# Streaming block with 64 routed experts: the expert sort is issued ahead of the shared expert, and the kinds of expert take another order

## What is computed

```
scores = sigmoid(t @ w_router)                      # 256 tokens x 64 experts
sel = scores + router_bias
grp_score = sum(top_k(sel in 8 groups of 8, 2))     # the best 4 groups may be used
idx = top_k(where(group allowed, sel, -inf), 8)     # 8 experts for each token
w = scores[idx] / sum(scores[idx]) * 2.5
out = (silu(t @ ws_gate) * (t @ ws_up)) @ ws_down   # shared expert, every token
for e in range(64):
    hid = silu(t @ we_gate[e]) * (t @ we_up[e])     # 1024 -> 256
    out = out + gates[:, e] * (hid @ we_down[e])    # 256 -> 1024
```

## Time and profile before

| | |
|---|---|
| median of 3 runs | 725.2 us (724.77 to 726.61) |
| the profiled execution, its own time | 724.93 us |
| its span, first to last instruction | 723.2 us |
| PE busy | 653.7 us, 90% |
| DVE, ACT, POOL busy | 294.0, 133.1, 38.8 us |
| mean granted TensorE clock | 0.985 of full |
| DMA | 250.70 MB, mean 347 GB/s |

### The profile page before, as it was taken

How to read it: one execution, slowest core, us unless ns; L and a number is a source line. 1 busy time by engine, 2 the same in 40 slices (tenths; PEclk the granted TensorE clock), 3 DMA queues, 4 the chain that set the end, 5 groups by cost and what they waited for, 6 DMA issues and landing times.

```text
span 723.2 us, 11178 instructions
## 1 busy us (share of the span) xinstructions
PE 653.7 (90%) x4223; PEld 380.0 (53%) x4223; DVE 294.0 (41%) x780; ACT 133.1 (18%) x282; POOL 38.8 (5%) x220
## 2 busy tenths in 40 slices
PE   0479999999978889999999999999999999999992
PEld 0448877844534454545545455554555545555541
DVE  4649987596462133233132331332323323232115
ACT  3501122121501111111111111111111111111112
POOL 7000000001100000000000000000000000000000
PEclk9999999999989999999999999999999999999996
DMA  7998789614419787999999999999999999999941
GB/s 238 395 389 323 246 323 411 255 58 175 174 58 421 284 320 282 421 423 420 420 420 421 420 419 420 421 420 421 420 420 420 419 421 420 422 419 420 421 202 60
DMA packets 46008, 250.70 MB, mean 347 GB/s; under 512 B 4673, under 2 KB 7809, under 8 KB 20993
## 3 DMA queue, kind: packets, MB, share of 16 engines
q1 hardware_dynamic: 44434, 248.59, 84.9%
q10 hardware_dynamic: 1520, 1.39, 0.6%
HBM read 248.91 MB, written 1.05 MB: 346 GB/s over the span
## 4 chain that ended last, share of the span: by engine, by line
PE 70%; DVE 17%; DMA 8%; ACT 2%; issue 1%; ACTq 1%; SPq 0%; DVEq 0%
PE PS L1517 10%; PE PS L1513 10%; PE PS L1496 9%; PE PS L1523 8%; DVE MOD L854 7%; PE PS L1571 5%; PE PS L1545 5%; PE PS L1549 5%; DMA ring<-in_w_ada_dram 5%; PE PS L1554 4%; DMA ring<-in_we_up_dram 3%; PE PS L1567 3%; PE PS L1532 2%; PE PS L1314 1%; PE PS L1442 1%
## 5 line engine op out<-in xcount | busy, mean ns | idle before, releaser
L1169 DVE SCALAR_TENSOR_TENSOR arena<-arena,gate,PS 128x128 f32<-128x128 f32 (+1 forms) x48 | 18.0, 375 | 172.6 <-ACT arena L769 172.6
L1314 PE MATMUL PS<-hT,ring 128*128 128x256 f32 x384 | 84.7, 380 | 0.0
L1517 PE MATMUL PS<-ring,arena 128*64 128x256 f32 x704 | 84.6, 391 | 0.0
L1180 DVE TENSOR_TENSOR YLO<-PS,YHI 128x512 fp32r<-128x512 f32 x58 | 40.1, 691 | 101.5 <-ACT YHI L780 101.5
L1314 PEld LDWEIGHTS PS<-hT,ring 128*128 128x128 f32 x384 | 72.5, 190 | 11.1 <-issue 1.6
L1496 PE MATMUL PS<-G,H2HI 128*128 128x256 f32 (+2 forms) x272 | 71.1, 297 | 7.8 <-ACT arena L760 7.2
L1513 PE MATMUL PS<-ring,arena 128*128 128x512 f32 x160 | 73.7, 612 | 0.7 <-issue 0.7
L854 DVE SCALAR_TENSOR_TENSOR MOD<-ring,ccol,MOD 128x768 f32<-128x768 f32 (+2 forms) x72 | 66.9, 930 | 12.5 <-ACT MOD L646 6.8
L780 ACT CAST YHI<-PS 128x512 fp32r<-128x512 f32 x58 | 34.0, 586 | 176.7 <-PE PS L1549 71.0
L1496 PE MATMUL PS<-G,H2LO 128*128 128x256 f32 (+2 forms) x272 | 66.2, 279 | 0.0
L1517 PEld LDWEIGHTS PS<-ring,arena 128*64 128x64 f32 x704 | 47.6, 134 | 31.9 <-issue 3.7
(11 more groups left out here) (255 smaller groups left out, 630.5 us busy)
## 6 DMA issues: line engine op xcount, KB each, us to landing
ring<-in_we_gate_dram SPq DMA_DIRECT2D x64, 1024.0 KB, 14.9
ring<-in_we_up_dram SPq DMA_DIRECT2D x64, 1024.0 KB, 18.1
ring<-in_we_down_dram SPq DMA_DIRECT2D x64, 1024.0 KB, 15.9
ring<-in_w_ada_dram SPq DMA_DIRECT2D x5, 3072.0 KB, 11.3
ring<-in_w_in_dram SPq DMA_DIRECT2D x3, 3072.0 KB, 18.0
ring<-in_w_ada_dram SPq DMA_DIRECT2D x4, 1536.0 KB, 16.0
ring<-in_w_out_dram SPq DMA_DIRECT2D x1, 3072.0 KB, 18.6
ring<-in_w_ada_dram SPq DMA_DIRECT2D x1, 2048.0 KB, 26.6
```

What stands on the lines that cost most here:

```text
L1180: dve.tensor_tensor(y_part(YLO, p, h), bank(5), y_part(YHI, p, h).bitcast(F32), ALU.subtract).then_inc(ylo_ready, 1)
L1314: mm = pe.matmul(PS[:, 2 + q % QB, 0:TOK], w[:, k, (m % 6) * P:(m % 6) * P + P], hT[:, k, :], start=(k == 0), stop=(k == KD - 1))
L1517: m = pe.matmul(PS[64 * c:64 * c + 64, 6, 0:FE].rearrange("p (a n) -> p a n", a=2), xt[:, k, :], gu_cols(w[0], k, c), start=(k == 0), stop ...
```

## The change

Four things are edited.

1. **Router and sort move forward.** On PE the second half's logits go ahead of the last eighth of `shared_gate_up(0)` and of the modulation rows; the counts (`rank_ps`) go into the middle of `shared_gate_up(1)`, and the matmul of the sort stands ahead of both `shared_down`. On ACT the sigmoid goes ahead of the first silu. On DVE the gate values, formerly between mask and ranks, go behind the sort, and `shared_hidden(1)` too.
2. **Units.** The two fixed wide experts are each followed by a pair (two units [wide, pair]); in the other units the wide expert comes last. The same kinds and numbers of positions remain.
3. **Ring.** A slot is handed on in the order in which the positions use it, and the start order of slots is 2, 3, 0, 4, 1 in place of 2, 3, 0, 1, 4.
4. **POOL.** It copies all `rankm` columns of a unit first, then (for the first unit after the new semaphore `rt_ready`) all `RT` columns, and reads the expert number from `order` once for either, twice in all.

Three of the four gather steps of the first unit now stand ahead of `shared_down(1)`.

```diff
-UNITS = ([[WIDE] * FIXED, [PAIR, PAIR]]
-         + 2 * (2 * [[WIDE, PAIR, NARROW], [WIDE, NARROW, PAIR], [NARROW, PAIR, NARROW]] + [[NARROW, PAIR, NARROW]])
+UNITS = (FIXED * [[WIDE, PAIR]]
+         + 2 * (2 * [[PAIR, NARROW, WIDE], [NARROW, PAIR, WIDE], [NARROW, PAIR, NARROW]] + [[NARROW, PAIR, NARROW]])
          + [[NARROW, NARROW]])
...
+PROC = [q for qs in EXPERTS for q in qs]
+POS_OF = [p for q in range(NE) for p in range(NPOS) if q in EXPERTS[p]]
+SLOT, USE = [2, 3, 0, 4, 1], [1] * NSLOT
+for q in range(NSLOT, NE):
+    SLOT.append(SLOT[PROC[q - NSLOT]])
+    USE.append(USE[PROC[q - NSLOT]] + 1)
... SP
                 if q >= NSLOT:
-                    sp.wait_ge(gu_done, POS_OF[q - NSLOT] + 1)
+                    sp.wait_ge(gu_done, POS_OF[PROC[q - NSLOT]] + 1)
... POOL
             for i in range(len(UNITS)):
-                if staged(i):
+                if i:
                     pool.wait_ge(slot_ps, i)
-                    for u, q in enumerate(of_unit(i)):
-                        col = bass.ds(pool.value_load(order[0:1, q - FIXED:q - FIXED + 1], min_val=0, max_val=NE - 1), 1)
-                        pool.tensor_copy(rcur[:, :, u:u + 1], rankm[:, :, col]).then_inc(cur_copied, 1)
-                        pool.tensor_copy(rtcur[:, :, u:u + 1, :], RT[:, :, col, :]).then_inc(cur_copied, 1)
+                for u, q in enumerate(of_unit(i)):
+                    if q >= FIXED:
+                        pool.tensor_copy(rcur[:, :, u:u + 1], rankm[:, :, number(q)]).then_inc(cur_copied, 1)
+                if i == 0:
+                    pool.wait_ge(rt_ready, 3)
+                for u, q in enumerate(of_unit(i)):
+                    if q >= FIXED:
+                        pool.tensor_copy(rtcur[:, :, u:u + 1, :], RT[:, :, number(q), :]).then_inc(rt_copied, 1)
... ACT
-            shared_silu(0)
-            copy_mod_rows(range(6, 8))
             act.wait_ge(logit_ps, TT)
             act.activation(score, PS[:, 7, 0:TT * NE].rearrange("p (t e) -> p t e", t=TT),
                            ACT.Sigmoid).then_inc(score_ready, 1)
-
+            shared_silu(0)
+            copy_mod_rows(range(6, 8))
... DVE
-            gather_matrix(0)
-            sort_experts()
+            sort_experts()
+            shared_hidden(1)
+            gather_matrix(0)
+            link(dve.tensor_tensor(gates, score, maskf, ALU.mult))
...
+            for part_no in range(3):
+                rt = RT[:, :, :, 1 + part_no]
+                link(dve.tensor_copy(rt, gates), rt_ready)
+                if part_no < 2:
+                    link(dve.tensor_tensor(gates, gates, rt, ALU.subtract))
             one_hots(0)
... PE
             h2_transposes(1)
-            shared_gate_up(0, range(5, KD))
+            shared_gate_up(0, range(5, 7))
+            logits(1)
+            shared_gate_up(0, range(7, KD))
             for r in range(6, 8):
                 mod_rows(r)
-            logits(1)
-            shared_hidden_transposes(0)
-            shared_gate_up(1, range(KD))
+            shared_gate_up(1, range(0, 5))
 
             pe.wait_ge(mask_ready, 1)
...
+            shared_gate_up(1, range(5, KD))
+            shared_hidden_transposes(0)
+            pe.wait_ge(sort_in, 2)
+            pe.matmul(PS[0:1, 7, PICK_COL:PICK_COL + NE - FIXED + 1], idcol[0:NE, :], pick[0:NE, :], start=True,
+                      stop=True).then_inc(order_ps, 1)
             pe.wait_ge(modrow_ready, 8)
             shared_down(0)
             shared_hidden_transposes(1)
-            pe.wait_ge(sort_in, 2)
-            pe.matmul(PS[0:1, 7, PICK_COL:PICK_COL + NE - FIXED + 1], idcol[0:NE, :], pick[0:NE, :], start=True,
-                      stop=True).then_inc(order_ps, 1)
+            pe.wait_ge(shid_ready, TT)
+            gather(0, range(0, 1))
+            pe.wait_ge(shT_ready, TT)
+            gather(0, range(1, 3))
             shared_down(1)
-            pe.wait_ge(shid_ready, TT)
-            pe.wait_ge(shT_ready, TT)
-            gather(0, range(4))
+            gather(0, range(3, 4))
+            pe.wait_ge(rt_ready, 3)
             pe.wait_ge(order_ready, 2)
             slot_values(0)
```

More of the change, by code:

```diff
@@ L62 @@
 ROWS = {WIDE: 128, NARROW: 64, PAIR: 32}
-EXPERTS = [list(range(sum(N_EXP[k] for k in KIND[:p]), sum(N_EXP[k] for k in KIND[:p + 1]))) for p in range(NPOS)]
-POS_OF = [p for p in range(NPOS) for _ in EXPERTS[p]]
+EXPERTS = []
+for p, kind in enumerate(KIND):
+    if p < 2 * FIXED and kind == WIDE:
+        EXPERTS.append([p // 2])
+    else:
+        first = max([FIXED - 1] + [q for qs in EXPERTS for q in qs]) + 1
+        EXPERTS.append(list(range(first, first + N_EXP[kind])))
+PROC = [q for qs in EXPERTS for q in qs]
[4 more added lines that the diff above has]
+    USE.append(USE[PROC[q - NSLOT]] + 1)
 NWIDE = KIND.count(WIDE) - FIXED
@@ L610, in _, with number @@
             pool.wait_ge(order_ready, 2)
+            def number(q):
+                return bass.ds(pool.value_load(order[0:1, q - FIXED:q - FIXED + 1], min_val=0, max_val=NE - 1), 1)
             for i in range(len(UNITS)):
-                if staged(i):
+                if i:
                     pool.wait_ge(slot_ps, i)
-                    for u, q in enumerate(of_unit(i)):
-                        col = bass.ds(pool.value_load(order[0:1, q - FIXED:q - FIXED + 1], min_val=0, max_val=NE - 1), 1)
-                        pool.tensor_copy(rcur[:, :, u:u + 1], rankm[:, :, col]).then_inc(cur_copied, 1)
-                        pool.tensor_copy(rtcur[:, :, u:u + 1, :], RT[:, :, col, :]).then_inc(cur_copied, 1)
+                for u, q in enumerate(of_unit(i)):
[6 more added lines that the diff above has]
+                        pool.tensor_copy(rtcur[:, :, u:u + 1, :], RT[:, :, number(q), :]).then_inc(rt_copied, 1)
         @block.scalar
@@ L1075, in _ @@
             link(dve.tensor_copy(maskb, maskf), mask_ready)
[L1076 to L1088, removed]
             dve.wait_ge(rank_ps, 1)
@@ L1181, in y_low @@
                                   ALU.subtract).then_inc(ylo_ready, 1)
+            sort_experts()
+            shared_hidden(1)
             gather_matrix(0)
-            sort_experts()
+            link(dve.tensor_tensor(gates, score, maskf, ALU.mult))
+            link(dve.tensor_reduce(grank[:, :, 0:1], gates, AX.X, ALU.add))
+            link(dve.reciprocal(grank[:, :, 0:1], grank[:, :, 0:1]))
+            for t in range(TT):
+                link(dve.tensor_scalar(gates[:, t, :], gates[:, t, :], grank[:, t, 0:1], ROUTED_SCALE,
+                                       ALU.mult, ALU.mult))
+            for part_no in range(3):
[3 more added lines that the diff above has]
+                    link(dve.tensor_tensor(gates, gates, rt, ALU.subtract))
             one_hots(0)
@@ L1508, in gate_up @@
                 for q in EXPERTS[p]:
-                    pe.wait_ge(gu_loaded[e_slot(q)], 32 * (q // NSLOT + 1))
-                w = [gu_w(e_slot(q)) for q in EXPERTS[p]]
+                    pe.wait_ge(gu_loaded[SLOT[q]], 32 * USE[q])
+                w = [gu_w(SLOT[q]) for q in EXPERTS[p]]
                 for k in range(KD):
@@ L1539, in down @@
                     for q in EXPERTS[p]:
-                        pe.wait_ge(down_loaded[e_slot(q)], 16 * (q // NSLOT + 1))
+                        pe.wait_ge(down_loaded[SLOT[q]], 16 * USE[q])
                 pe.wait_ge(ylo_ready, parts_before(p) + half)
-                w = [down_w(e_slot(q)) for q in EXPERTS[p]]
+                w = [down_w(SLOT[q]) for q in EXPERTS[p]]
                 for cc in range(FT):
```

31 lines of the change are left out of this document (15 added, 16 removed).

## The result

The changed kernel takes 712.3 us (median of 4 runs, 711.4 to 713.4), the kernel before 725.0 (4 runs). The ratio is 0.982, 95% interval 0.980 to 0.984: faster by 12.7 us, 1.8%. The forecast was 710.5 us with a range of 708.0 to 716.5.

What follows compares the result with a forecast made beforehand. The prediction took PE to set the end, with the weights' stream in balance some microseconds ahead. Terms -5.4, -1.3, -5.2, -1.4 and -1.2 made -14.5: 724.93 to 710.5 us, range 708.0 to 716.5.

Steps and rivals of the forecast that it cites:

- (a): Around the sort: the list stands earlier and the first routed product starts at 217.2 in place of 222.57, -5.4 us.
- (b): Second wide expert's down: a pair in its place has one half, so its YLO wait goes, -1.3 us.
- (c): Gather steps: waits go at eight wide positions, -6.1 us; first units get worse; -5.2 us in all.
- (d): PE clock after 240 to 244 us: stays up instead of falling to half, -1.4 us, otherwise 0.
- this rival: First two units: the clock still falls, once giving 711.9 us, at both places 713.3; chance 0.2.
- Stream: Weight loads: holes shrink to 7.5 from 16.2 us, so PE's transfer wait near the end all but vanishes, -1.2 us.
- (e): Costs of nothing: POOL's second read of the list, 5.2 us a unit, is hidden beside PE; uncovered, 2.1 us a unit.
- the rival with YLO late: Wide positions: DVE's G and one-hot block delays YLO past 1.9 us of cover; 727.3 us with 4 more; chance 0.04.
- signs set down beforehand: Expected traces of each term, among them granted clock 1.00 from 230 to 260 and under 9 us of holes before 280.
- The sign of being wrong: PE's routed part, first product to last `add_up`, shortens by less than 6 us, or transfer waits exceed 2 us.
- the estimate in the prediction: Sigmoid's table load: by the skill page's added drain, the sigmoid starts only at 194.6 and the time is 1.2 us longer.

Runs made afterwards that it cites:

- e1: Changed kernel with the units, experts and slots of before, so only the early sort is left (POOL's new copy order stays): 719.0 us, ratio 0.993.
- e7: Changed kernel with the units from the third on as before (wide expert first): 715.2 us, ratio 0.987.
- e5: Changed kernel with only the first half of the down weights loaded from expert 10 on (lighter stream, output invalid): 713.1 us, ratio 0.985.
- e4: Changed kernel with the gather steps of the second and third unit alternating between two PSUM banks: 705.7 us, ratio 0.973.
- e3: Changed kernel with the ring's start order of slots as before (2, 3, 0, 1, 4): 712.6 us, ratio 0.984.
- e6: Changed kernel with the first two units and the slots of before, leaving early sort and wide experts last: 719.8 us, ratio 0.993.
- e2: Kernel before with one edit, wide experts last in the units from the third on: 724.1 us, ratio 1.000.
- e8: Kernel before with wide experts last, and only half of the down weights loaded from expert 10 on (output invalid): 718.3 us, ratio 0.992.

## Why the prediction was right, and where it was off

The direction, the mechanism and the range held; 12.7 us faster for 14.5 forecast. That it came so near is in part luck: a term that gave more than forecast covers some of those that gave less. By its steps:

- **(a) Start of the routed experts, -5.4.** Measured -6.1. The chain ran as worked out: DVE's first step at 193.68 (forecast 193.7), `order` at 204.88, the idle time ahead of the sort 0.28 us (0.3), the second shared down 3.62 us (3.6). The counts waited 0.28 us for the mask. The missing 0.7 us lie mostly in the clock's part: for the second shared down the sum set 3.6 us, the product's whole duration, against 5.8, the distance to the next start. Like for like it is 3.62 against 6.39, 2.8 us and not 2.2. e1 shows the term alone by the medians: 5.7 us. A single execution isn't sharper than that: with the same start, the first routed product stands between 215.4 (e7) and 217.4 us (e5).
- **(b) -1.3.** The second YLO wait is gone. That at position 0 grew from 1.18 to 1.29.
- **(c) Gather steps, -5.2, was mis-sized.** A place was priced at 0.82 and 0.7 us, from a step that waits against one that is followed by an `add_up`. At position 0, with 192 columns, it is even 0.83 (4 steps in 3.68 us in e4 and 6.16 in e3, at full clock). At the eight wide positions it is less: 5.5 us from position 4 on, 0.69 a place, and 5.3 against e7, 0.66; forecast -6.1. Between the two steps that stood directly behind one another there is now the `add_up` of a pair or a narrow expert, and behind it the first matmul is as long as behind a wait (0.39 us; 0.28 inside a step), so the start-up isn't saved there. The changed kernel:

```profile
296.29 0.39 PE L1508 MATMUL PS<-G,H2HI 128*128 128x256 f32 x1
```

  In the first units (b) and this term together were forecast at -0.4 us; like for like they cost 0.6. The waits at position 0 rose from 1.44 us to 1.79, position 2 has a third one, and the rest isn't traced.
- **(d) Clock, -1.4, failed in the profiled execution.** It fell again, once, at nearly the same place. I had given this rival 0.2 and 711.9 us, and it is what came. The size was nearly right (a fall costs 1.7 us, last section), the assumption "stays up" was not.
- **Stream, -1.2.** Measured -1.26 (1.66 to 0.4). The holes were 9.4 us by the slices, 7.5 in my sum. The first units aren't needed for the small wait as such (0.6 us in e1, without them), but for keeping it small once PE saves time in (c): 6.8 us in e6 without them, 0.4 with them.
- **(e), and the rival with YLO late.** Of the wide positions only position 0 waited for YLO in the changed kernel. POOL's second read of the list held nobody up: DVE waited for POOL once, 1.49 us ahead of the first G and on the first read, hidden beside the first shared down, and PE never did.

The sum of the steps then reads -6.1 (a), +0.6 (b with the first units' part of c, clock as before), -5.5 (c at the wide positions) and -1.3 (transfer wait): -12.3, the difference of the spans. Against the forecast 1.4 us are missing for the clock, 1.0 in the first units and 0.6 at the wide positions; (a) gave 0.7 more.

Of the signs set down beforehand, two failed: the clock did not stay at 1.00 from 230 to 260 us, and the holes were 9.4 us, not under 9. The sign of being wrong was missed narrowly: PE's routed part, first product to last `add_up`, went from 487.3 to 481.2 us, 6.15 us shorter, where under 6 was to count as wrong and the sum had 9.1.

The prediction didn't see how much hangs on the order of the parts. It took (c) as saved by PE because the stream could follow. It can only with the new first units; on the kernel before the same edit is worth nothing (e2).

The sigmoid's table: the load took 1.28 us here too, and the sigmoid began 0.16 us behind it, when the logits came. ACT's timeline of the changed kernel:

```profile
191.86 1.28 ACT L758 ACT_TABLE_LOAD   x1
193.30 0.28 ACT L758 ACTIVATE arena<-PS 128x128 f32<-128x128 f32 x1 [0.16 <-PE PS L1423]
```

No drain is to be seen, and DVE began at 193.68, when the forecast from rows said. By the page "ScalarE: Activation LUTs" of the Trainium skill, section "What ACT_TABLE_LOAD costs", which adds a drain to each switch, it would have begun 1.2 us later, by the estimate in the prediction. The measurement decides.

## What to carry to other kernels

Where a compute engine and the stream of weights are in balance, an edit that saves compute time may be worth nothing until the stream has a lead: e2 saves 5 us of waits between gather steps and gets 5 us of transfer waits. Look for the lead where the stream has holes, early in the run, and try the edit again behind that; a run with a lighter stream tells in one go which of the two sets the end. And a row of short waits between steps that share one buffer costs more than its idle time: with two banks, six waits of together 3.9 us gave back 6.6 by the medians, of which in the profiled executions 1.7 were the clock, which may fall or not.

## What the runs showed of the hardware

**The half clock behind broken stretches comes and goes with the same work on PE.** Up to position 2 the kernels e3, e5, e7 and the changed one issue the same work on PE at nearly the same spacing. PE of e3:

```profile
234.82 0.36 PE L1508 MATMUL PS<-G,H2HI 128*128 128x192 f32 x1 [0.57 <-ACT arena L777]
...
235.79 1.90 PE L1557 MATMUL PS<-ring,arena 128*128 128x512 f32 x4
```

and its stretches:

```profile
230.00:234.00 4.00, 2.78 (x23) 2.44 (x22) 1.30 (x5) 0.48 (x1) 1.12 (x6) 1.00 1.02 420
234.00:239.00 5.00, 3.23 (x16) 1.79 (x14) 1.21 (x2) 1.23 (x3) 0.41 (x3) 1.00 1.01 421
```

The clock stays at 2.4 GHz, and the down product takes 1.90 us, where in the changed kernel it took 2.86 at 0.66. From the first routed product to position 4 the executions without a fall take 51.5 (e3) and 51.4 us (e7), those with one 53.2 (changed kernel) and 53.2 (e5): 1.7 us for a fall. Each of these is one execution; with the old first units (the kernel before, e1, e2, e6, e8) the clock fell between 234 and 250 us in all five. Such a stretch is a risk, not a fixed cost. In e4, which has no such waits, the clock stays up there, but one execution doesn't show that it always would.

Here the clock went down with PE busy two thirds of the time and no wait above 0.65 us. The page "TensorE: Matmul & The Clock Gate" of the Trainium skill, section "Part 1: The HAM clock gate", has the clock go down after idleness, which by itself would not explain this. The same part of the page, under "A second HAM failure mode: psum-queue depth-cycling", tells of a kernel in which frequent short idle spells between groups of matmuls made it swing between the two clocks, and this trace agrees with that. What decides between the two outcomes for the same work, these runs don't show.
